# FFN up in seven products: partial sums accumulated in PSUM onto ScalarE's copy of P1, and the hidden scale from ScalarE's sums of squares

## The reference, cut to what matters

```python
def swiglu(u, wg, wu, wd):
    return (jax.nn.silu(u @ wg) * (u @ wu)) @ wd
```

## Time and profile before

| | us |
|---|---|
| median of three runs (2235.79 to 2241.22) | 2240.34 |
| profiled execution, its own time | 2240.52 |
| its span, first to last instruction | 2238.7 |
| TensorE busy | 2005.8 |
| VectorE busy | 1525.6 |
| ScalarE busy | 1020.5 |
| GpSimd busy | 743.7 |

### The profile page before, as it was taken

The page is one execution under the profiler, slowest core; times in us unless marked ns, Lnnn a source line. Parts: engine busy times, 40 slices in busy tenths (PEclk is TensorE's granted clock), DMA queues, the critical chain, the costliest instruction groups (busy, mean ns, idle before and its releaser), DMA issues. The chain is left out here.

```text
span 2238.7 us, 34927 instructions
## 1 busy us (share of the span) xinstructions
PE 2005.8 (90%) x13896; PEld 1506.3 (67%) x13896; DVE 1525.6 (68%) x2314; ACT 1020.5 (46%) x1114; POOL 743.7 (33%) x446
## 2 busy tenths in 40 slices
PE   3899999999998788879999996999999678999999
PEld 2677667665776655657767774776677455776777
DVE  7888963314987644288898348889853778889732
ACT  5566653102153244155666334566643225666621
POOL 5666500000037403056661014665300426655000
PEclk9999999997999878999999998999999879999999
DMA  3222222210121011012222211222222201322221
GB/s 130 76 94 98 97 104 78 79 53 10 57 66 52 16 76 38 0 48 99 99 75 97 104 66 52 97 94 87 97 105 71 77 3 57 112 92 78 104 101 46
DMA packets 24023, 167.05 MB, mean 75 GB/s; under 512 B 3024, under 2 KB 3024, under 8 KB 8176
## 3 DMA queue, kind: packets, MB, share of 16 engines
q1 hardware_dynamic: 22176, 157.98, 20.4%
q0 software_dynamic: 1744, 7.66, 1.0%
HBM read 161.80 MB, written 3.83 MB: 74 GB/s over the span
## 5 line engine op out<-in xcount | busy, mean ns | idle before, releaser
L1633 PE MATMUL ps<-big 128*128 128x296 f16 x2464 | 719.2, 292 | 98.4 <-DVE big L1083 34.3
L1637 PE MATMUL ps<-big 128*128 128x296 f16 x2464 | 718.0, 291 | 6.4 <-DVE big L966 6.0
L1634 PE MATMUL ps<-big 128*128 128x296 f16 x2464 | 718.4, 292 | 0.0
L1614 PE MATMUL ps<-big 128*128 128x296 f16 x4224 | 538.3, 290 | 10.5 <-DVE big L1066 10.5
L1614 PEld LDWEIGHTS ps<-big 128*128 128x128 f16 x4224 | 410.4, 98 | 132.6 <-DVE big L1066 11.7
L1633 PEld LDWEIGHTS ps<-big 128*128 128x128 f16 x2464 | 242.4, 98 | 192.4 <-DVE big L1088 42.6
L381 POOL TENSOR_TENSOR big<-big 128x512 f32<-128x512 f32 x88 | 125.5, 1426 | 735.4 <-ACT big L555 396.7
L566 ACT ACTIVATE big<-big,scales 128x1536 f16<-128x1536 f32 x88 | 138.8, 1577 | 397.7 <-PE ps L1637 204.6
L1637 PEld LDWEIGHTS ps<-big 128*128 128x128 f16 x2464 | 242.7, 99 | 83.3 <-DVE big L966 12.6
L1608 PE MATMUL ps<-big 128*128 128x296 f32 x992 | 263.3, 428 | 35.9 <-DVE big L1543 26.7
L1634 PEld LDWEIGHTS ps<-big 128*128 128x128 f16 x2464 | 242.9, 99 | 67.3
(11 more groups left out here) (267 smaller groups left out, 2157.5 us busy)
## 6 DMA issues: line engine op xcount, KB each, us to landing
big<-in_w_up SPq DMA_DIRECT2D x88, 1024.0 KB, 4.8
big<-in_w_dn SPq DMA_DIRECT2D x32, 1408.0 KB, 6.0
big<-in_w_in SPq DMA_DIRECT2D x20, 512.0 KB, 3.5
big<-in_w_out SPq DMA_DIRECT2D x1, 4096.0 KB, 12.3
resid<-in_x SPq DMA_DIRECT2D x4, 592.0 KB, 6.8
out_y<-resid SPq DMA_DIRECT2D x8, 296.0 KB, 4.4
big<-in_w_ai POOLq DMA_DIRECT2D x1, 2048.0 KB, 10.7
big<-in_w_pool POOLq DMA_DIRECT2D x1, 1024.0 KB, 5.2
```

Of the source, the lines that this page charges most:

```text
L1614: last = mm(ps[:, bank + hf, 0:HALF], w, x[:, hf * HALF:(hf + 1) * HALF], start=start, stop=stop)
L1633: mm(out, w[:, 0, c], xop[:, 0, x, c], start=start, stop=False, skip_group_check=True)
L1634: mm(out, w[:, 1, c], xop[:, 0, x, c], start=False, stop=False, skip_group_check=True)
L1637: last = mm(out, w[:, 0, c], xop[:, 1, x, c], start=False, stop=(c == DC // 2 - 1), skip_group_check=True)
```

## The change

- ScalarE copies P1 not to SBUF but into the bank of P6 (`seed_p1`), and P6, P7 and P4 accumulate onto it. So the bank holds u2 after P6, u3 after P7 and c21 after P4. At the start of the program two matmuls with `start=True` write banks 1 and 4 once. `FAST` takes P5 ahead of P6, which now waits for the seed.
- u2 is copied out by ScalarE (`keep_u2`); VectorE makes c22 from PSUM (`sum_c22`) and c12; c21 is read straight from PSUM by a second Silu (`silu_second`) and a second product (`hidden_second`). `silu_rest` and `hidden_rest` are left with two blocks of four.
- The scale for FFN down comes from sums of squares: ScalarE's `hidden_rows`, one per pair, in place of VectorE's maximum. It is read from the total by halving its exponent, as for the weights.
- P1 waits only for `wlow1_done`; P5 waits for `wlow_done`. In the first pair, the first half's P6 moves ahead of the second half's P3, and the products behind it alternate. Stage 0's totals of the first two steps move from banks 4 and 5 to 3 and 5.
- In VectorE's turn low2 stands right behind low1.

```diff
-FAST = "P1", "P6", "P5", "P2", "P7", "P3", "P4"
+FAST = "P1", "P5", "P6", "P2", "P7", "P3", "P4"
 FIRST = "P1", "P2", "P5", "P3", "P6", "P7", "P4"
 PRODUCTS = {"P1": (0, 0, 0), "P2": (1, 1, 0), "P5": (3, 2, 2), "P3": (6, 3, 2),
             "P6": (4, 4, 1), "P7": (5, 5, 1), "P4": (2, 6, 1)}
-BEGINS = "P1", "P5", "P6"
+BEGINS = "P1", "P5"
...
+            def seed_p1(f, i, b, order):
+
+                product_of(f, i, b, order, "P1")
+                if later(f, i):
+                    act.wait_ge(hid2_done if b else silu2_done, i + PAIRS * f)
+                a.activation(ps[:, 3 * b + 1, 0:HALF], ps[:, 3 * b, 0:HALF], ACT.Copy).then_inc(p1_done[b], 1)
...
+            def keep_u2(f, i, b, order):
+
+                product_of(f, i, b, order, "P6")
+                if later(f, i):
+                    act.wait_ge(hid_done if b else silu_done, i + PAIRS * f)
+                a.activation(tmp[:, b, 0], ps[:, 3 * b + 1, 0:HALF], ACT.Copy).then_inc(u2_done[b], 1)
...
+            def silu_second(f, i, order):
+
+                act.wait_ge(wback_done, 2 * i + f * FFN_UNITS + 1)
+                product_of(f, i, 0, order, "P4")
+                if later(f, i):
+                    act.wait_ge(hid2_done, i + PAIRS * f)
+                a.activation(act4[:, 2], ps[:, 1, 0:HALF], ACT.Silu, scale=wback[:, 0:1]).then_inc(silu2_done, 1)
...
+            def hidden_rows(f, i):
+
+                for done in (hid1_done, hid2_done, hid_done):
+                    act.wait_ge(done, i + PAIRS * f + 1)
+                act.wait_ge(rows_done, f * FFN_UNITS + 1)
+                if later(f, i):
+                    act.wait_ge(hpart_done, i + PAIRS * f)
+                a.activation(hjunk, hid_half[:, bass.ds(4 * i + 4, 4), :].rearrange("p a n -> p (a n)"), ACT.Square,
+                             accum_out=hmax[:, bass.ds(i, 1)]).then_inc(hpart_done, 1)
...
                 step_high1(stage, 2 * i + 1, 1)
-                keep_p1(f, i, 0, FAST)
+                seed_p1(f, i, 0, FAST)
                 step_high2(stage, 2 * i + 1, 1)
                 keep_p5(f, i, 0, FAST)
+                keep_u2(f, i, 0, FAST)
                 bound(stage, 2 * i + 2, 0, DN_W if last_turn else STEP_W)
+                hidden_rows(f, i - 1)
                 silu_first(f, i, FAST)
                 for c in head[:1]:
                     act.wait_ge(hscale_done, 2 * f + 1)
                     hidden_high(f, c, 0)
+                if not last_turn:
+                    step_high1(stage, 2 * i + 2, 0)
+                seed_p1(f, i, 1, FAST)
                 if last_turn:
                     down_high(stage, FC, 0)
                 else:
-                    step_high1(stage, 2 * i + 2, 0)
-                keep_p1(f, i, 1, FAST)
-                silu_rest(f, i)
-                if not last_turn:
                     step_high2(stage, 2 * i + 2, 0)
                 keep_p5(f, i, 1, FAST)
+                keep_u2(f, i, 1, FAST)
+                silu_second(f, i, FAST)
+                silu_rest(f, i)
                 bound(stage, 2 * i + 3, 1, DN_W if last_turn else STEP_W)
...
-                for q in range(4, 7):
-                    x_highs(f, q)
+                x_highs(f, 4)
+                x_highs(f, 5)
+                keep_u2(f, 0, 0, FIRST)
+                x_highs(f, 6)
+                keep_u2(f, 0, 1, FIRST)
                 bound(stage, 3, 1)
                 step_high1(stage, 2, 0)
+                silu_second(f, 0, FIRST)
...
+                hidden_rows(f, PAIRS - 1)
                 down_high(stage, FC + 1, 1)
...
+            def sum_c22(f, i, b, order):
 
                 dve.wait_ge(prod_done[b], 7 * i + 7 * PAIRS * f + order.index("P7") + 1)
-                v.tensor_tensor(tmp[:, b, 2], ps[:, 3 * b + 1, 0:HALF], tmp[:, b, 1], ALU.add).then_inc(u3_done[b], 1)
-
-            def sum_c22(f, i, b):
                 dve.wait_ge(p5_done[b], i + PAIRS * f + 1)
-                dve.wait_ge(u3_done[b], i + PAIRS * f + 1)
-                v.tensor_tensor(tmp[:, b, 2], tmp[:, b, 2], tmp[:, b, 3], ALU.add)
+                v.tensor_tensor(tmp[:, b, 1], ps[:, 3 * b + 1, 0:HALF], tmp[:, b, 1], ALU.add).then_inc(c22_done[b], 1)
 
             def sum_c12(f, i, b, order):
                 dve.wait_ge(prod_done[b], 7 * i + 7 * PAIRS * f + order.index("P3") + 1)
                 dve.wait_ge(u2_done[b], i + PAIRS * f + 1)
-                v.tensor_tensor(tmp[:, b, 0], ps[:, 3 * b + 2, 0:HALF], tmp[:, b, 0], ALU.add)
-
-            def sum_c21(f, i, b):
-                dve.wait_ge(prod_done[b], 7 * i + 7 * PAIRS * f + 7)
-                v.tensor_tensor(tmp[:, b, 1], ps[:, 3 * b + 1, 0:HALF], tmp[:, b, 1], ALU.add).then_inc(c_done[b], 1)
+                v.tensor_tensor(tmp[:, b, 0], ps[:, 3 * b + 2, 0:HALF], tmp[:, b, 0], ALU.add).then_inc(c12_done[b], 1)
...
+            def hidden_second(f, i):
+
+                dve.wait_ge(silu2_done, i + PAIRS * f + 1)
+                dve.wait_ge(prod_done[1], 7 * i + 7 * PAIRS * f + 7)
+                dve.wait_ge(wback_done, 2 * i + f * FFN_UNITS + 2)
+                h = hid_half[:, bass.ds(4 * i + 6, 1), :].rearrange("p a n -> p (a n)")
+                v.scalar_tensor_tensor(h, ps[:, 4, 0:HALF], wback[:, 1:2], act4[:, 2], ALU.mult, ALU.mult) \
+                    .then_inc(hid2_done, 1)
...
-                    sum_c21(f, i - 1, 1)
+                    hidden_second(f, i - 1)
+                    sum_c12(f, i - 1, 1, FAST if not isinstance(i, int) or i > 1 else FIRST)
                     hidden_rest(f, i - 1)
+                    dve.wait_ge(hid1_done, i + PAIRS * f)
+                    dve.wait_ge(hid2_done, i + PAIRS * f)
                     dve.wait_ge(hid_done, i + PAIRS * f)
                     weight_back(stage, 2 * i + 1, 1, ix)
                     step_low1(stage, 2 * i + 1, 1)
-                    sum_u2(f, i, 0, FAST)
-                    hidden_pair_max(f, i - 1)
+                    step_low2(stage, 2 * i + 1, 1)
+                    sum_c22(f, i, 0, FAST)
                     if after_max:
                         after_max()
-                    step_low2(stage, 2 * i + 1, 1)
-                    sum_u3(f, i, 0, FAST)
-                    sum_c22(f, i, 0)
+                    if not last_turn:
+                        weight_scale(stage, 2 * i + 2, 0)
+                    sum_c12(f, i, 0, FAST)
                     for c in head[:1]:
                         hidden_low(c, 0)
-                    sum_c12(f, i, 0, FAST)
-                    if not last_turn:
-                        weight_scale(stage, 2 * i + 2, 0)
-                    sum_c21(f, i, 0)
                     if last_turn:
                         weight_scale(stage, FC, 0)
-                        sum_u2(f, i, 1, FAST)
                         down_low(stage, FC, 0)
                     else:
                         step_low1(stage, 2 * i + 2, 0)
-                        sum_u2(f, i, 1, FAST)
                         step_low2(stage, 2 * i + 2, 0)
-                        dve.wait_ge(silu_done, i + PAIRS * f + 1)
+                    sum_c22(f, i, 1, FAST)
+                    hidden_first(f, i, FAST)
+                    if not last_turn:
+                        for done in (silu1_done, silu2_done, silu_done):
+                            dve.wait_ge(done, i + PAIRS * f + 1)
                         weight_back(stage, 2 * i + 2, 0, ix)
-                    hidden_first(f, i, FAST)
-                    sum_u3(f, i, 1, FAST)
-                    sum_c22(f, i, 1)
                     for c in head[1:]:
                         hidden_low(c, 0)
-                    sum_c12(f, i, 1, FAST)
                     if not last_turn:
                         weight_scale(stage, 2 * i + 3, 1)
...
                     if name == "P1":
+                        pe.wait_ge(wlow1_done, 2 * i + b + f * FC + 1)
+                    if name == "P5":
                         pe.wait_ge(wlow_done, 2 * i + b + n0 + 2 + 1)
-                    first_pair = isinstance(i, int)
-                    if name in BEGINS and not first_pair:
-                        pe.wait_ge((silu1_done if b == 0 else hid1_done) if name == "P1" else c_done[b], at)
-                    if name == "P2":
+                    first_pair = isinstance(i, int) and i == 0
+                    if name == "P1" and not first_pair:
+                        pe.wait_ge(hid1_done if b else silu1_done, at)
+                    if name == "P5" and not first_pair:
+                        pe.wait_ge(c12_done[b], at)
+                    if name in ("P2", "P6"):
                         pe.wait_ge(p1_done[b], at + 1)
                     if name == "P3":
                         pe.wait_ge(p5_done[b], at + 1)
                     if name == "P7":
                         pe.wait_ge(u2_done[b], at + 1)
                     if name == "P4":
-                        pe.wait_ge(u3_done[b], at + 1)
+                        pe.wait_ge(c22_done[b], at + 1)
...
```

(6 more changed lines are left out.)

93 lines of the change are left out of this document (43 added, 50 removed).

## The result

| | before | after |
|---|---|---|
| median of the runs, us | 2240.78 (4 runs) | 2177.13 (4 runs: 2172.58 to 2178.14) |
| ratio, with its 95% interval | | 0.9712 [0.9686, 0.9738] |
| profiled execution: its time, its span | 2240.5, 2238.7 | 2178.1, 2176.4 |

The kernel is 63.7 us faster. Forecast were 47.4 us (2193) and a range of 2182 to 2214: the sign is right, and the gain is a third larger than forecast, 5 us beyond the range.

A forecast was written before the change was run, and what follows sets the result against it. TensorE, busy 2005.8 of 2238.7 us, was taken to wait for short VectorE adds behind long splits, VectorE being late rather than saturated. 32 + 16.4 - 1.0 = 47.4 us off 2240.5 gave 2193; range 2182 to 2214.

The forecast's parts named there:

- term (a): From the second half of pair 1 on: TensorE's waits on u3, u2 and the P1 copy go; gain 32 us.
- the steps: Timeline of one pair on ScalarE, VectorE and TensorE: seeds and u2 copies each ready 0.7 to 0.8 us early.
- rivals 1: ScalarE's squares as slow as three maxima, 4.1 us, pushing high1, seed and bound; gain gone, 2238 us; chance 0.03.
- 3: Seed: ScalarE's copy into PSUM is slow; at 1.9 to 2.0 us the kernel takes about 2264 us; chance 0.05.
- rival 2: Hand-overs worse than the timeline: register waits and GpSimd's hold on VectorE eat the 0.7 us slacks; 2214 us; chance 0.15.
- rival 4: More than forecast: no rest in hidden-chunk pairs, no 1.2 us seed wait in pair 1; 2181 us; chance 0.12.
- (b): First pair and first half of pair 1: reordered products run without the 3.78 us hole; gain 16.4 us.
- (c): End of FFN up: total of the hidden scale 0.25 us later, moving hidden splits and down_low; -1.0 us over four FFNs.

The follow-up runs named there:

- the dead copies: Kernel after with a dead ScalarE copy ahead of each seed, of 592 elements (0.69 us) or 1184 (1.18 us): 2179.16 and 2216.35 us.

## Why the prediction was too low

**What failed is a size: the length of the waits in term (a).** The mechanism was right. VectorE was late and not saturated; every operation stands in the trace where the steps had it; rivals 1 (squares 1.37 us, not 4.1) and 3 (seed 0.40, slack shown by the dead copies) are out, and so is rival 2: its slacks were used up only by 1.18 us more. The time went past rival 4's 2181, but not by rival 4's way: in pairs 7 to 10 the rest came as forecast, and of pair 1's 1.2 us for the seed 0.93 were there. By stages the gain is 14.6 us over the forecast: 11.7 in (a), 4.7 in (b), 1.8 less in (c).

**Term (a), forecast 32, measured 43.7.** Its first number was "about 40 from start to start": I took FFN 0's 8.8 us for all, 35, and added 5 for gaps that the rows count short. In the kernel before, 64 steps from one matmul's start to the next are over 0.3 us there, and they exceed a plain step of 0.126 by 48.8 us. The lists of waits show 45 of them with 36.5 us (9.0, 8.9, 10.5 and 8.1 by FFN), so that taking FFN 0 for all cost little. The 5 should have been 12: each listed wait is 0.16 longer from start to start, as the row of 1.90 with its gap of 2.06 showed, which is 7, and 19 short ones stand in no list, 5 more. The second number was the rest, "rounded to 8": what is left is 4.9, in 9 steps. All of them are in pairs 8 and 9, where 4.8 were forecast for pairs 7 to 10; the early pairs lose nothing of the 2.0 forecast there, and the rounding added 1.2. An example of such a rest is the step from pair 8 to 9, in the rows below: VectorE's hidden rests and scale hold high1 back until 242.25 (ScalarE idles 2.93 us), and TensorE waits 0.55 us for the seed behind it (0.67 and 0.56 at the same place of FFN 1 and 3):

```profile
238.67 3.08 DVE L1185 SCALAR_TENSOR_TENSOR big<-big,scales 128x592 f16<-128x592 f32 x2
...
242.16 0.53 DVE L1150 SCALAR_TENSOR_TENSOR big<-ps,scales,act_out 128x296 f32<-128x296 f32 x1
```

```profile
242.25 1.58 ACT L569 ACTIVATE big<-big,scales 128x1536 f16<-128x1536 f32 x1 [2.93 <-DVE scales L1092]
```

**Term (b), forecast 16.4, measured 21.0** (to the last P4 of pair 1's first half: 4.0, 5.25, 5.2 and 6.5). FFN 2 starts 32.42 us later in the kernel before; in the times of the earlier trace rows, P1 was forecast at 1393.9 and came at 1393.2; P5 at 1397.0, came at 1396.3; P6 at 1399.7, came at 1398.9. The 0.8 is `bound`, done 0.4 sooner, and low1, 2.15 us there and not 2.58: the row is from a place where GpSimd works beside it. The rest is FFN 3, 1.3 more: in the kernel before its matmuls ran at half the granted clock behind the hole of 3.78 us for 7 more matmuls than in FFN 2, and I had priced all by FFN 2.

**Term (c), forecast -1.0, measured -2.8**: FFN down is 0.27 us longer in each FFN at either of its two lengths, 1.1 in all, which is the size forecast. The wait for its second unit stayed at 2.6 us. New is one near its start, where TensorE's total of the hidden scale waits for VectorE's sum of ScalarE's squares:

```profile
PE ps L1615 <- DVE scales L1170: 1.5, 4, 0.4
```

What I did not foresee is that it has two lengths, 1.65 us apart: the kernel before shows the longer in 2 of 4, the kernel after in 3, and that makes the 2.8 us lost.

**The rule weighed.** By the earlier trace rows I took ScalarE's squares as cheap as VectorE's maximum. Measured are 1.18 + 0.19 us against 1.37: the rows hold, and the squares alone are worth 20 us. The Trainium skill (ScalarE: Activation LUTs, Rules for kernel authors) would have max, add and mul on VectorE, which it calls up to about 3 times faster in bf16. No run here is in bf16; in fp32 these rows show no such advantage for this sum.

**The range.** Its lower end was rival 4 alone. The two unknowns, the length of the waits and what is left of them, were both taken on the careful side, and the first could be read. The steps from start to start alone (48.8 less 8 is 41, not 32) would have given 2184, and 2171 with rival 4's 13 us below it.

## What to carry to other kernels

A wait in a list is shorter than what it costs: count from start to start of the instructions around it, for every wait of every stage, before pricing its removal. Where two engines hand over by turns, ask what the chain's slack is and not how busy the engine is: a dead instruction of known length in front of the hand-over measures it. A hole in the matmuls can cost more behind itself than by itself: one of 4.2 us in place of three that add up to 3.7 lost 2.1 to 3.2 us per FFN. And a part of a change that is worth nothing by itself can be worth 9 us once another part has made room; test parts by taking them out as well as by putting them in.
